# Two products in one 512-column matmul, and modulation sums along VectorE's free axis

## The chip, the cores and the metric

The kernel runs on one NeuronCore of a Trainium2 chip, in one launch. The metric is device time in microseconds (us), the median of several runs of the same program. The engines are called TensorE (PE in the profile, PEld for its weight loads), VectorE (DVE), ScalarE (ACT), GpSimd (POOL) and SyncE (SP, which here issues all loads and stores).

## The reference

Two layers over 256 tokens of width 2048. Each layer takes six modulation vectors from a condition vector, mixes the tokens (layer 0: mLSTM and forgetting attention; layer 1: gated linear attention), and applies a feed-forward block with a convolution over three tokens.

```python
cond = jax.nn.silu(c)
for layer in range(DEPTH):
    mod = (cond @ ada_w[layer] + ada_b[layer])[:, None, :]
    sh_m, sc_m, g_m, sh_f, sc_f, g_f = jnp.split(mod, 6, axis=-1)
    h = rms_norm(x, norm_w[layer, 0]) * (1.0 + sc_m) + sh_m
    y = even_mixer(h, ...) if layer % 2 == 0 else odd_mixer(h, ...)
    x = x + g_m * rms_norm(y, norm_w[layer, 1])
    h = rms_norm(x, norm_w[layer, 2]) * (1.0 + sc_f) + sh_f
    y = conv_ffn(h, ffn_in_w[layer], ffn_conv_w[layer], ffn_conv_b[layer], ffn_out_w[layer])
    x = x + g_f * rms_norm(y, norm_w[layer, 3])

def conv_ffn(h, w_in, conv_w, conv_b, w_out):
    u = h @ w_in                     # 2048 -> 11264
    u = conv over 3 tokens per channel + conv_b
    a, g = jnp.split(u, 2, axis=-1)
    return (a * jax.nn.gelu(g, approximate=True)) @ w_out   # 5632 -> 2048
```

All of it is fp32. `ada_w` is 2 x 2048 x 12288, the largest single weight beside the feed-forward ones.

## The kernel before

Activations lie transposed, channels on the 128 partitions and the 256 tokens (`T`) along the free axis. Every dense product is done with operands split into a high part (rounded to fp32r) and a low part (the remainder): weight-hi times activation-hi, weight-hi times activation-lo, weight-lo times activation-hi. The activation of one channel tile is one row of `act` (or `mid` in the second feed-forward product) with hi in columns 0 to 255 and lo in 256 to 511.

Weights come in 402 units of 1 MB (128 x 2048 floats). A unit of the kinds gates, columns, mixed, ff_up and ff_down is 16 weight tiles of 128 x 128 that make one output tile of 128 channels x 256 tokens; in the last ff_down group of each layer it is 12 tiles. That makes 370 such units; the other 32, of the kind values, use the activations as the stationary operand and 512 weight columns as the moving one. Four raw slots hold loaded units, two slots each of `hi` and `lo` the split ones. For unit n+1 ScalarE writes `hi` (L440, once TensorE has ended unit n-1, whose slot it takes) and VectorE writes `lo` (L806), while TensorE works on unit n. VectorE then evacuates unit n from PSUM (L1186, L1189, L1192; in ff_up the convolution, L1201, L1204 and L1208). Bank 0 and bank 2 alternate.

The order of the work is written out by hand: `PHASES` lists the stages, and in each the loop over units is the same on every engine, in program order. Beside the stages run side jobs (the heads of fox, mlstm and gla), and the modulation: `ada_w` is loaded in 384 pieces of 512 KB, 128 input channels x 1024 outputs each. VectorE multiplies a piece by the 128 conditions (one scalar per partition) and adds it into `acc` (L819 for the first two of a section, L820 for the others). 32 pieces make a section, one of the 12 modulation vectors. Then `reduce_section` sums over the partitions on TensorE, with 16 matmuls of `acc` against a column of ones (L1263), and `close_section` adds the bias (L824). The first 64 pieces are done in a head before the first unit; the others are spread over the units by the tuple `ada` of each stage: one per unit in ff_up (all of layer 0 and the first group of layer 1, 120 units), three per two units in most others, none in the later stages of layer 1. They go through two slots (`piece`).

In ff_up two further engines work on the product: ScalarE applies gelu (L681), GpSimd multiplies (L787), ScalarE rounds to `mid` hi (L685) and GpSimd subtracts (L790) to get `mid` lo.

## Time and profile before

| | |
|---|---|
| median of 3 runs | 2718.58 us (2718.3 to 2723.91) |
| span of the profiled execution | 2725.8 us |
| TensorE busy | 2538.6 us, 93% |
| VectorE busy | 2017.8 us, 74% |
| ScalarE busy | 1076.9 us, 40% |
| GpSimd busy | 460.7 us, 17% |
| loaded | 626.42 MB, 231 GB/s over the span |

The profile is one execution; no total time is given for it apart from its span, which runs from its first to its last instruction. Matmuls overlap each other in the records, so the sum over matmul rows is more than TensorE's busy time, and a matmul's price in a stream is the distance between starts. Other engines' operations are recorded with their duration, and the distance between starts can be a little shorter. "x32" in a row is the number of instructions merged in it.

### The profile page before, as it was taken

Reading aid. Unit: us, or ns where it says so; the run is one execution under the profiler, and the core shown is the slowest. Engines: PE = TensorE matmul, PEld = TensorE weight load, DVE = VectorE, ACT = ScalarE, POOL = GpSimd, SP = SyncE. Lnnn points to the kernel's source line nnn. Section 1 sums busy time; section 2 is a strip of 40 time slices with the busy share of each in tenths; the row PEclk is TensorE's granted clock in tenths of the full one; section 3 lists DMA queues with packets and bytes.
Section 4 is the critical chain, followed back from the end, with each engine's and each line's share of the span. In section 5 each row is a group of like instructions: output and inputs, shape, how many; then the busy total and the mean of one; then the engine's idle time right before and its main releaser. Section 6 shows DMA issues by size and latency. Waiting matters only on the chain.

```text
span 2725.8 us, 48585 instructions
## 1 busy us (share of the span) xinstructions
PE 2538.6 (93%) x19382; PEld 2460.2 (90%) x19382; DVE 2017.8 (74%) x1998; ACT 1076.9 (40%) x1111; POOL 460.7 (17%) x230
## 2 busy tenths in 40 slices
PE   2599998989999999999989999989999999999997
PEld 2498877979999999999988989989899999999997
DVE  7876876789977799688777676667999456645655
ACT  1333334454433333233455544444533334333444
POOL 0100000013420244013301000000344014411320
PEclk7699989989999999999999999989999999999998
DMA  9887764747768767787665644357477455445543
GB/s 394 319 312 272 276 229 147 264 184 263 277 250 309 266 256 276 269 296 261 239 232 215 236 152 151 143 207 272 175 270 265 169 185 185 180 177 183 185 172 137
DMA packets 114640, 630.38 MB, mean 231 GB/s; under 512 B 12736, under 2 KB 12864, under 8 KB 62928
## 3 DMA queue, kind: packets, MB, share of 16 engines
q1 hardware_dynamic: 114512, 628.57, 63.0%
q8 instruction: 93, 1.52, 0.2%
q14 instruction: 35, 0.29, 0.0%
HBM read 626.42 MB, written 2.10 MB: 231 GB/s over the span
## 4 chain that ended last, share of the span: by engine, by line
PE 79%; DVE 9%; DMA 6%; ACT 3%; issue 2%; POOL 0%; DVEq 0%; SPq 0%; ACTq 0%; POOLq 0%
PE bank L1437 23%; PE bank L1438 22%; PE bank L1439 22%; DMA piece<-ada_pieces 4%; DVE acc L820 3%; PE bank L1456 2%; PE bank L1458 2%; PE bank L1457 2%; PE bank L1263 2%; DMA region<-ada_pieces 2%; DVE lo L806 1%; ACT hi L440 1%; PE bank L1341 1%; DVE act L865 1%; PE bank L1256 1%
## 5 line engine op out<-in xcount | busy, mean ns | idle before, releaser
L440 ACT ACTIVATE hi<-raw 128x2048 fp32r<-128x2048 f32 x402 | 769.6, 1915 | 1365.4 <-PE bank L1439 1238.0
L1437 PE MATMUL bank<-act,hi 128*128 128x256 f32 x4384 | 1266.8, 289 | 42.3 <-DVE act L865 26.1
L1438 PE MATMUL bank<-act,hi 128*128 128x256 f32 x4384 | 1252.7, 286 | 0.0
L1439 PE MATMUL bank<-act,lo 128*128 128x256 f32 x4384 | 1252.4, 286 | 0.0
L806 DVE TENSOR_TENSOR lo<-raw,hi 128x2048 fp32r<-128x2048 f32 x402 | 920.2, 2289 | 186.6 <-ACT hi L440 185.4
L1437 PEld LDWEIGHTS bank<-act,hi 128*128 128x128 f32 x4384 | 854.5, 195 | 52.6 <-issue 37.6
L1438 PEld LDWEIGHTS bank<-act,hi 128*128 128x128 f32 x4384 | 854.9, 195 | 1.0
L1439 PEld LDWEIGHTS bank<-act,lo 128*128 128x128 f32 x4384 | 854.0, 195 | 0.0
L820 DVE SCALAR_TENSOR_TENSOR acc<-piece,cond,acc 128x1024 f32<-128x1024 f32 x300 | 436.9, 1458 | 84.3 <-DMA piece<-ada_pieces 83.7
L1437 PE MATMUL bank<-mid,hi 128*128 128x256 f32 x1408 | 408.7, 290 | 12.3 <-POOL mid L790 11.2
L1438 PE MATMUL bank<-mid,hi 128*128 128x256 f32 x1408 | 402.2, 286 | 0.0
L1439 PE MATMUL bank<-mid,lo 128*128 128x256 f32 x1408 | 402.0, 286 | 0.0
L787 POOL TENSOR_TENSOR region<-region 128x256 f32<-128x256 f32 x88 | 201.9, 2294 | 733.4 <-ACT region L681 733.4
L1437 PEld LDWEIGHTS bank<-mid,hi 128*128 128x128 f32 x1408 | 274.4, 195 | 14.4 <-POOL mid L790 12.0
L1438 PEld LDWEIGHTS bank<-mid,hi 128*128 128x128 f32 x1408 | 274.3, 195 | 0.8
L1439 PEld LDWEIGHTS bank<-mid,lo 128*128 128x128 f32 x1408 | 274.1, 195 | 0.0
L790 POOL TENSOR_TENSOR mid<-region,mid 128x256 f32 (+1 forms) x88 | 206.9, 2352 | 291.2 <-ACT mid L685 291.2
L1201 DVE TENSOR_SCALAR region<-bank,vec 128x256 f32<-128x256 f32 x176 | 95.3, 542 | 118.0 <-PE bank L1439 113.3
L743 POOL TENSOR_SCALAR region<-y,mod 128x256 f32<-128x256 f32 x16 | 25.8, 1614 | 557.6 <-DVE y L856 557.6
L1456 PE MATMUL bank<-hi,act 128*128 128x512 f32 x256 | 102.2, 399 | 2.0 <-DVE lo L806 2.0
L1457 PE MATMUL bank<-lo,act 128*128 128x512 f32 x256 | 99.8, 390 | 0.0
L1204 DVE SCALAR_TENSOR_TENSOR region<-bank,vec,region 128x255 f32<-128x255 f32 x176 | 85.0, 483 | 19.9 <-DVE region L1201 1.9
(155 smaller groups left out, 1612.0 us busy)
## 6 DMA issues: line engine op xcount, KB each, us to landing
raw<-w_units SPq DMA_DIRECT2D x402, 1024.0 KB, 4.8
piece<-ada_pieces SPq DMA_DIRECT2D x320, 512.0 KB, 4.9
region<-ada_pieces SPq DMA_DIRECT2D x64, 512.0 KB, 8.6
x<-x_in SPq DMA_DIRECT2D x1, 2048.0 KB, 15.0
x_out<-x SPq DMA_DIRECT2D x4, 512.0 KB, 2.6
vec<-vectors SPq DMA_DIRECT2D x1, 542.5 KB, 3.7
extra<-blocks_in SPq DMA_DIRECT2D x1, 512.0 KB, 18.9
causal<-causal_in SPq DMA_DIRECT2D x1, 256.0 KB, 18.1
```

What stands on the lines that cost most here:

```text
L440: sc.activation(hi[:, slot, :], raw[:, raw_slot, :], ACT.Copy).then_inc(s_hi, 1)
L787: gp.tensor_tensor(ff_m[:, slot, :], conv_a[:, slot, :], gelu_g[:, slot, :], ALU.mult).then_inc(s_mul, 1)
L790: gp.tensor_tensor(flat(mid[:, at_, T:2 * T]), ff_m[:, slot, :], flat(mid[:, at_, 0:T].bitcast(F32)), ALU.subtract).then_inc(s_mid, 1)
L806: ve.tensor_tensor(lo[:, slot, :], raw[:, raw_slot, :], hi[:, slot, :].bitcast(F32), ALU.subtract).then_inc(s_lo, 1)
L820: return ve.scalar_tensor_tensor(out=at_, in0=src, scalar=weight, in1=at_, op0=ALU.mult, op1=ALU.add)
L1201: ve.tensor_scalar(out_, tile_ps, vec[:, bass.ds(ch + 2, 1)], vec[:, bass.ds(ch + 3, 1)], ALU.mult, ALU.add).then_inc(s_v, own.tick())
L1204: ve.scalar_tensor_tensor(out=out_[:, 1:T], in0=tile_ps[:, 0:T - 1], scalar=vec[:, bass.ds(ch + 1, 1)], in1=out_[:, 1:T], op0=ALU.mult, op ...
L1437: pe.matmul(dst, w_hi, src[:, kt, 0:T], start=at == 0, stop=False)
L1438: pe.matmul(dst, w_hi, src[:, kt, T:2 * T], start=False, stop=False)
L1439: i_ = pe.matmul(dst, w_lo, src[:, kt, 0:T], start=False, stop=at == len(order) - 1)
L1456: pe.matmul(dst, x_hi, w_hi, start=kt == 0, stop=False)
L1457: pe.matmul(dst, x_hi, w_lo, start=False, stop=False)
```

## The change

Three things are changed together. In the 370 units that make 128-channel tiles, weight-hi is multiplied with the whole 512-column row of the activation (hi and lo side by side) in one matmul into a whole PSUM bank; weight-lo times activation-hi is added to the first half. The second half is copied to a new tile `low` by ScalarE (`stage_low`) and added by VectorE while it evacuates. Second, the modulation weights are laid out with the output channels on the partitions, `cond` is the condition vector along the free axis, copied to all partitions, and one VectorE operation per piece multiplies and sums into one column of `part`. Third, the one-column matmuls go; `close_section` adds the two halves of each sum and the bias on VectorE.

```diff
-            sc.wait_ge(s_in["vec"], 16)
-            sc.activation(cond[:, :], vec[:, V_C:V_C + DK], ACT.Silu).then_inc(s_cond, 1)
+            sc.wait_ge(s_in["c"], 16)
+            sc.activation(cond[:, :], cond[:, :], ACT.Silu).then_inc(s_cond, 1)
+
+            def stage_low(ph, i, j):
+                t = ph.t0 + j
+                sc.wait_ge(s_unit, SPLIT_SLOTS + unit(ph, i, j) + 1)
+                sc.wait_ge(s_evac, 2 + t + i * ph.tiles)
+                sc.activation(low[:, :], bank[2 * (t % 2)][:, T:2 * T], ACT.Copy).then_inc(s_low, 1)
...
+                        if ph.kind != "values" and not (ph.side == "mlstm" and j == 3):
+                            stage_low(ph, i, j)
...
-            def summed(src, half, kt, first, acc=acc):
-                at_, weight = acc[:, half * PIECE:(half + 1) * PIECE], cond[:, bass.ds(kt, 1)]
-                if first:
-                    return ve.tensor_scalar(at_, src, weight, None, ALU.mult)
-                return ve.scalar_tensor_tensor(out=at_, in0=src, scalar=weight, in1=at_, op0=ALU.mult, op1=ALU.add)
+            def summed(src, half, at_):
+                return ve.scalar_tensor_tensor(out=src, in0=src, scalar=1.0, in1=cond[:, half * PIECE:(half + 1) * PIECE],
+                                               op0=ALU.mult, op1=ALU.mult, accum_out=part[:, bass.ds(at_, 1)])
             def close_section(sec):
-                ve.wait_ge(s_red, sec + 1)
-                ve.tensor_tensor(mod[:, sec, :], bank[7][:, 0:DK], vec[:, V_ADAB + sec * DK:V_ADAB + (sec + 1) * DK],
+                two = part[:, sec % 2 * PIECES:(sec % 2 + 1) * PIECES].rearrange("p (k two) -> p k two", two=2)
+                ve.wait_ge(s_mac, (sec + 1) * PIECES)
+                ve.tensor_tensor(mod[:, sec, :], two[:, :, 0], two[:, :, 1], ALU.add).then_inc(s_pair, 1)
+                ve.wait_ge(s_pair, sec + 1)
+                ve.tensor_tensor(mod[:, sec, :], mod[:, sec, :], vec[:, V_ADAB + sec * DK:V_ADAB + (sec + 1) * DK],
                                  ALU.add).then_inc(s_mod, 1)
...
-                        ve.wait_ge(s_mac, a - 1)
...
                         elif ph.kind == "columns":
-                            ve.tensor_copy(region[:, bass.ds((ph.dest + ph.units * i + j) * T, T)], tile_ps)\
+                            ve.tensor_tensor(region[:, bass.ds((ph.dest + ph.units * i + j) * T, T)], tile_ps, low[:, :],
+                                             ALU.add).then_inc(s_evac, 1)
...
                         elif ph.kind == "ff_down":
                             at_ = flat(y[:, bass.ds(4 * i + j, 1), :])
-                            ve.tensor_tensor(at_, at_, tile_ps, ALU.add).then_inc(s_evac, 1)
+                            ve.tensor_tensor(low[:, :], at_, low[:, :], ALU.add).then_inc(s_v, own.tick())
+                            mine()
+                            ve.tensor_tensor(at_, tile_ps, low[:, :], ALU.add).then_inc(s_evac, 1)
                         elif ph.kind == "ff_up":
...
-                            ve.tensor_scalar(out_, tile_ps, vec[:, bass.ds(ch + 2, 1)], vec[:, bass.ds(ch + 3, 1)],
+                            ve.tensor_tensor(low[:, :], tile_ps, low[:, :], ALU.add).then_inc(s_v, own.tick())
+                            mine()
+                            ve.tensor_scalar(out_, low[:, :], vec[:, bass.ds(ch + 2, 1)], vec[:, bass.ds(ch + 3, 1)],
                                              ALU.mult, ALU.add).then_inc(s_v, own.tick())
                             mine()
-                            ve.scalar_tensor_tensor(out=out_[:, 1:T], in0=tile_ps[:, 0:T - 1],
+                            ve.scalar_tensor_tensor(out=out_[:, 1:T], in0=low[:, 0:T - 1],
...
-            def reduce_section(sec, acc=acc):
-                if sec > 0:
-                    pe.wait_ge(s_mod, sec)
-                pe.wait_ge(s_mac, (sec + 1) * PIECES)
-                for j in range(DK):
-                    i_ = pe.matmul(bank[7][:, j:j + 1], acc[:, j * P:(j + 1) * P], ones[:, 0:1], start=True, stop=True)
-                i_.then_inc(s_red, 1)
...
-                        pe.matmul(dst, w_hi, src[:, kt, 0:T], start=at == 0, stop=False)
-                        pe.matmul(dst, w_hi, src[:, kt, T:2 * T], start=False, stop=False)
-                        i_ = pe.matmul(dst, w_lo, src[:, kt, 0:T], start=False, stop=at == len(order) - 1)
+                        pe.matmul(both, w_hi, src[:, kt, :], start=at == 0, stop=False)
+                        i_ = pe.matmul(both[:, 0:T], w_lo, src[:, kt, 0:T], start=False, stop=at == len(order) - 1)
...
-    ada = ada_w.reshape(LAYERS, DK, P, 6, 2, PIECE).transpose(0, 3, 1, 4, 2, 5).reshape(-1, P, PIECE)
+    ada = ada_w.reshape(LAYERS, 2, PIECE, 6, DK, P).transpose(0, 3, 4, 1, 5, 2).reshape(-1, P, PIECE)
```

Left out: the copy of c is now the first load (1 MB, from one row of 8 KB), and `vec` comes after the head's first eight pieces; VectorE waits for `low` (`s_low`) before an evacuation, not for TensorE; the phases count their column units; the other evacuations are changed like the one shown.

The program's order on VectorE in ff_up with a piece, before, from one split (`lo`) to the next; region is where the convolution's result lies:

```order
L806 TENSOR_TENSOR lo<-raw,hi 128x2048
L820 SCALAR_TENSOR_TENSOR acc<-piece,cond,acc 128x1024
L1201 TENSOR_SCALAR region<-bank,vec 128x256
L1204 SCALAR_TENSOR_TENSOR region<-bank,vec,region 128x255
L1208 SCALAR_TENSOR_TENSOR region<-bank,vec,region 128x254
```

and at the same place after the change:

```order
L818 TENSOR_TENSOR lo<-raw,hi 128x2048
L829 SCALAR_TENSOR_TENSOR piece,part<-piece,cond 128x1024
L1218 TENSOR_TENSOR low<-bank,low 128x256
L1220 TENSOR_SCALAR region<-low,vec 128x256
L1223 SCALAR_TENSOR_TENSOR region<-low,vec,region 128x255
L1227 SCALAR_TENSOR_TENSOR region<-low,vec,region 128x254
```

Five operations are six now, and the last three read `low` instead of the bank.

On ScalarE, in the straight part at the end of an ff_up stage, before (hi is a split, the L681 row a gelu):

```order
L440 ACTIVATE hi<-raw 128x2048
L681 ACTIVATE region<-region 128x256
L440 ACTIVATE hi<-raw 128x2048
L685 ACTIVATE mid<-region 128x256
L440 ACTIVATE hi<-raw 128x2048
```

and after:

```order
L442 ACTIVATE hi<-raw 128x2048
L691 ACTIVATE region<-region 128x256
L686 ACTIVATE low<-bank 128x256
L442 ACTIVATE hi<-raw 128x2048
L695 ACTIVATE mid<-region 128x256
L686 ACTIVATE low<-bank 128x256
L442 ACTIVATE hi<-raw 128x2048
```

Each unit has a `low` copy, behind gelu or the rounding and ahead of the split of the unit after next.

On TensorE, inside an ff_up stage of layer 0 where a section ends, before (ones is the column of ones, acc the sums):

```order
L1437 MATMUL bank<-act,hi 128x256
L1438 MATMUL bank<-act,hi 128x256
L1439 MATMUL bank<-act,lo 128x256
L1263 MATMUL bank<-ones,acc 128x1 x16
L1437 MATMUL bank<-act,hi 128x256
```

After the change the rows named L1263 are gone, and every tile reads (here the first two tiles of the first unit):

```order
L1443 MATMUL bank<-act,hi 128x512
L1444 MATMUL bank<-act,lo 128x256
L1443 MATMUL bank<-act,hi 128x512
L1444 MATMUL bank<-act,lo 128x256
```

## Rows read from the trace of the kernel before

**Rows 1.** The page's busy time per engine, share of the span and instructions.

```profile
PE 2538.6 (93%) x19382; PEld 2460.2 (90%) x19382; DVE 2017.8 (74%) x1998; ACT 1076.9 (40%) x1111; POOL 460.7 (17%) x230
```

**Rows 2.** Stretches: length, busy PE, PEld, DVE, ACT, POOL, PEclk, DMA, GB/s.

```profile
642.00:665.00 23.00, 23.00 (x194) 23.00 (x193) 21.58 (x21) 9.06 (x9) 9.48 (x4) 1.00 0.74 274
2206.00:2390.00 184.00, 184.00 (x1536) 184.00 (x1535) 118.64 (x125) 71.23 (x62) 69.16 (x29) 1.00 0.50 182
```

**Rows 3.** Timeline of ScalarE, two units of columns and two of values: start, duration.

```profile
129.31 1.92 ACT L440 ACTIVATE hi<-raw 128x2048 fp32r<-128x2048 f32 x1 [3.84 <-PE bank L1439]
135.07 1.92 ACT L440 ACTIVATE hi<-raw 128x2048 fp32r<-128x2048 f32 x1 [3.84 <-PE bank L1439]
...
234.88 1.92 ACT L440 ACTIVATE hi<-raw 128x2048 fp32r<-128x2048 f32 x1 [3.52 <-PE bank L1458]
240.32 1.92 ACT L440 ACTIVATE hi<-raw 128x2048 fp32r<-128x2048 f32 x1 [3.52 <-PE bank L1458]
```

**Rows 4.** Groups by line and shape: count, busy us, mean ns, idle before.

```profile
L1437 PE MATMUL bank<-act,hi 128*128 128x256 f32 x4384 | 1266.8, 289 | 42.3 <-DVE act L865 26.1 <-DVE act L1082 12.7 <-DVE lo L806 3.2
L1437 PE MATMUL bank<-mid,hi 128*128 128x256 f32 x1408 | 408.7, 290 | 12.3 <-POOL mid L790 11.2 <-DVE lo L806 1.1
L1189 DVE COPY y<-bank 128x256 f32 x40 | 16.9, 423 | 27.8 <-PE bank L1439 27.8
L1192 DVE TENSOR_TENSOR y<-y,bank 128x256 f32<-128x256 f32 x32 | 13.4, 420 | 35.0 <-PE bank L1439 35.0
L934 DVE TENSOR_SCALAR region<-region,stat 128x256 f32<-128x256 f32 x24 | 7.4, 350 | 0.4
L594 ACT ACTIVATE region<-bank 128x256 f32<-128x256 f32 x4 | 1.5, 374 | 1.3 <-PE bank L1268 1.3
L1003 DVE CUSTOM_DVE_ANT_0 region<-region,bank 128x256 f32<-128x256 f32 x8 | 3.0, 416 | 0.0
L1003 DVE DVE_READ_ACCUMULATOR2_ANT stat<- 128x1 f32 x8 | 0.7, 84 | 0.0
```

**Rows 5.** The one-column matmuls: their group, and those of one section end.

```profile
L1263 PE MATMUL bank<-ones,acc 128*128 128x1 f32 x352 | 52.7, 284 | 29.0 <-DVE acc L820 29.0
...
940.30 4.19 PE L1263 MATMUL bank<-ones,acc 128*128 128x1 f32 x32 [0.41 <-DVE acc L820]
```

**Rows 6.** Waits: total us, times, longest us.

```profile
PE bank L1263 <- DVE acc L820: 29.0, 8, 22.2
DVE mod L824 <- PE bank L1263: 19.1, 8, 4.3
```

**Rows 7.** Timeline of VectorE: a unit of ff_up in the loop; below, straight code.

```profile
649.26 2.28 DVE L806 TENSOR_TENSOR lo<-raw,hi 128x2048 fp32r<-128x2048 f32 x1
651.46 1.76 DVE L820 SCALAR_TENSOR_TENSOR acc<-piece,cond,acc 128x1024 f32<-128x1024 f32 x1
653.20 0.55 DVE L1201 TENSOR_SCALAR region<-bank,vec 128x256 f32<-128x256 f32 x1
653.89 0.48 DVE L1204 SCALAR_TENSOR_TENSOR region<-bank,vec,region 128x255 f32<-128x255 f32 x1
654.52 0.48 DVE L1208 SCALAR_TENSOR_TENSOR region<-bank,vec,region 128x254 f32<-128x254 f32 x1
654.99 2.29 DVE L806 TENSOR_TENSOR lo<-raw,hi 128x2048 fp32r<-128x2048 f32 x1
...
934.32 0.53 DVE L1201 TENSOR_SCALAR region<-bank,vec 128x256 f32<-128x256 f32 x1
934.89 0.48 DVE L1204 SCALAR_TENSOR_TENSOR region<-bank,vec,region 128x255 f32<-128x255 f32 x1
```

**Rows 8.** Timeline of GpSimd beside that unit.

```profile
649.73 2.41 POOL L790 TENSOR_TENSOR mid<-region,mid 128x256 f32 x1 [3.37 <-ACT mid L685]
```

**Rows 9.** Timeline of the head: ScalarE's Silu, VectorE's sums.

```profile
4.47 0.22 ACT L676 ACTIVATE cond<-vec 128x16 f32<-128x16 f32 x1 [2.46 <-DMA vec<-vectors]
21.98 28.04 DVE L820 SCALAR_TENSOR_TENSOR acc<-region,cond,acc 128x1024 f32<-128x1024 f32 x22 [5.34 <-DMA region<-ada_pieces]
```

More of the change, by code:

```diff
@@ L75, in place @@
         pairs += 2 * self.bodies if self.kind == "ff_up" else 0
-        return self.end, t + self.bodies * self.tiles, self.a_end, pairs
+        c += 0 if self.kind == "values" else self.bodies * self.units
+        return self.end, t + self.bodies * self.tiles, self.a_end, pairs, c
     def straight(self, i):
@@ L139 @@
 REGION = V_AT + TB * D
-OWN = {("ff_up", None): 8, ("columns", "fox"): 6, ("values", "fox"): 12, ("columns", "mlstm"): 14,
+OWN = {("ff_up", None): 12, ("columns", "fox"): 6, ("values", "fox"): 12, ("columns", "mlstm"): 14,
        ("values", "gla"): 8, ("columns", "gla"): 8}
@@ L223, in program @@
         ident = sb("ident", [P, P])
-        ones = sb("ones", [P, T])
+        ones = sb("ones", [P, P])
+        low = sb("low", [P, T])
         causal = sb("causal", [P, TB, T])
@@ L1152, in sum_piece @@
                         a = ph.a0 + i * ph.per_body + k
-                        done = (ph.a0 + ph.now * ph.per_body + k) % PIECES - ph.now * ph.per_body
-                        first = isinstance(a, int) and a % PIECES < 2
-                        if first and a % PIECES == 0 and (k > 0 or ph.side == "mlstm" or not first_body(i)):
+                        first = isinstance(a, int) and a % PIECES == 0
+                        if first and (k > 0 or ph.side == "mlstm" or not first_body(i)):
                             close_section(a // PIECES - 1)
@@ L1174, in body @@
                         tile_ps = bank[2 * (tile_no % 2)][:, 0:T]
-                        if ph.kind != "values" or j % 4 == 3:
+                        if ph.kind != "values":
+                            ve.wait_ge(s_low, ph.c0 + i * ph.units + j + 1)
+                        elif j % 4 == 3:
                             ve.wait_ge(s_unit, SPLIT_SLOTS + n + 1)
@@ L1214, in body @@
                         k += ph.ada[j]
-                per = OWN.get((ph.kind, ph.side), 0)
+                per = ph.units if ph.kind == "ff_down" and ph.group > 0 else OWN.get((ph.kind, ph.side), 0)
                 roots_per = 2 if ph.side == "mlstm" else 0
@@ L1416, in columns @@
                     pe.wait_ge(s_evac, ph.t0 + i * ph.tiles + j + 1)
-                    dst = bank[2 * ((ph.t0 + j) % 2)][:, 0:T]
+                    both = bank[2 * ((ph.t0 + j) % 2)][:, :]
                     src = mid if ph.kind == "ff_down" else act
@@ L1467, in body @@
                             {"fox": fox_work, "mlstm": mlstm_work, "decay": decay_work, "gla": gla_work}[ph.side](ph, i, j)
-                        a = ph.a0 + i * ph.per_body + sum(ph.ada[:j])
-                        if isinstance(a, int):
-                            for last in range(a, min(a + ph.ada[j], ph.a_end - 1)):
-                                if last % PIECES == PIECES - 1:
-                                    reduce_section(last // PIECES)
                         if ph.sums and not (first_body(i) and j == 0):
@@ L1589 @@
         "ada_pieces": np.ascontiguousarray(ada),
+        "c_row": np.ascontiguousarray(c),
         "vectors": vec,
```

56 lines of the change are left out of this document (24 added, 32 removed).

## The prediction

> **What bounds the kernel now.** I read the page's busy line first, then a table of stretches, then single units, then the operations one by one. The busy line gives TensorE 2538.6 us of 2725.8 [rows 1], so what TensorE has to stream is the first suspect, and a second engine has to be looked for stage by stage. The stretches do that [rows 2]. In the ff_up stage of layer 1 without modulation pieces TensorE is busy for all 184 us, VectorE for 118.6: TensorE bounds it, with a third of VectorE to spare. In the ff_up stage of layer 0, where every unit also sums a piece, TensorE is busy all the time too, but VectorE 21.58 of 23.00, 94%. There two engines are within 6% of each other, and work moved from one to the other shows at once.
>
> The unit times say what TensorE's stream costs. ScalarE's split of the unit after next starts when TensorE ends a unit. In the columns stage these starts lie 5.76 us apart, with 48 matmuls of 256 columns each: 120.0 ns a matmul. In the values stage they lie 5.44 us apart, with 24 matmuls of 512 columns: 226.7 ns [rows 3]. The same 12,288 columns go through in both, so a matmul costs 13.3 ns beside its columns, at the full clock.
>
> **Part 1, the merged matmul.** One 512-column matmul takes the place of two of 256: per weight tile 226.7 + 120.0 = 346.7 ns for 360.0, 13.3 less. A unit of 16 tiles goes from 5.76 to 5.55 us (0.21 less), one of 12 tiles loses 0.16. There are 4384 + 1408 = 5792 tiles [rows 4], 77 us in all, if TensorE bounds every unit. It doesn't:
> - 88 units of layer 1's ff_up and ff_down without pieces are bound by TensorE alone, 18.8 us; the 32 of 12 tiles give 5.1 us.
> - 96 units of the stages with three pieces in two units, and 34 of gates, fox, mlstm and gla, give 27.7 us if TensorE bounds them. Some wait for a piece to land, or for ScalarE and VectorE in a side job, so I take half, 13.8.
> - 120 units of ff_up with a piece (88 of layer 0, 32 of layer 1) give nothing; part 3 shows why.
>
> Together -37.7 us. The price of a mixed pair isn't in the trace; between nothing saved (a pair costs 360) and the 13.3 of a uniform stream I take the latter.
>
> By the Trainium skill ("TensorE: Matmul & The Clock Gate", section "Wait — 56ns, not 53.3ns?") a warm matmul costs only about 2.5 ns beside its columns. By that, all 5792 merges would be worth 14 us and the sum would end some 30 us higher. The rows show 13.3 ns here, and the measurement decides.
>
> **Part 2, the one-column matmuls.** A section's reduction is 16 of them, recorded as 32, and it stands in TensorE's stream: at 940.30 it takes 4.19 us, with 0.41 us of waiting for VectorE's last piece in front. Over eleven sections they are busy 52.7 us [rows 5], 4.8 each; I take 4.6, between the two rows. One of the eleven lies in the head, where TensorE has nothing else to do, and two (the ends of the mixed stages) beside the norm's own chain; there I count nothing. The other eight give 37 us. The waits in front are 29.0 us, of which the longest, 22.2, is the head's; 6.8 are left. VectorE in turn waits up to 4.3 us to close a section [rows 6], so neither engine covers the other and the time is real. -44 us. What replaces them is one more 128x16 add on VectorE, no more than 0.4 us a section with its wait.
>
> **Part 3, the evacuation.** The two correction products now lie in two halves of a bank, and someone has to add them. ScalarE copies the second half to `low` (a PSUM copy of 256 took 374 ns, L594 in [rows 4]), and VectorE adds. For columns, mixed and the first ff_down group the add replaces a copy that costs the same (423 ns against 420 for an add with one input in PSUM). In ff_down's later groups there is one more add. In ff_up there is one more add and one more wait in the chain of four.
>
> The ff_up unit with a piece, start to start now [rows 7]: 2.20 (split) + 1.74 (piece) + 0.69 + 0.63 + 0.47 = 5.73 us, which fills TensorE's 5.76. The piece takes 1.76 rather than 1.28 us, because GpSimd's add, started 0.47 us after the split, ends 0.68 us after the piece began [rows 7, 8]. Afterwards: an add of 0.42 plus the 0.15 that a dependent step waits in such a loop, +0.57. The `tensor_scalar` reads SBUF in place of PSUM (350 ns in L934 against 550), -0.19. The two others read SBUF, and their 480 ns is their price with a scalar from memory; unchanged. 5.73 + 0.57 - 0.19 = 6.11, and 0.04 for a collision now and then: 6.15 us. That is more than 5.55 and more than 5.76: VectorE becomes the bound, and 0.39 us x 120 units = +47 us. Bounds: if the waits cost only the 0.04 us seen in straight code (last two of [rows 7]), 5.95 us, +23. If every second unit's GpSimd add now collides a second time (its `mid` subtraction falls beside two-input SBUF operations, which it didn't before) for another 0.48, and the accumulator is read out for 0.08, 6.45 us, +83.
>
> The piece operation itself: it loses the scalar in memory and gains an accumulator. The nearest row is L1003, 416 ns for 256 elements and 84 ns for reading the accumulator, but the next one starts while it is read. I take no change for 1.28 us; from -0.06 to +0.25 as bounds, and a doubling is a rival below.
>
> **Part 4, what grows in latency.** ScalarE's `low` stands in front of the split of the unit after next: TensorE end, 0.4 for `low`, 1.92 split, 2.29 low part, near 4.8 us; through VectorE in ff_up 0.5 + 2.2 + 2.3 = 5.0. Both are below 5.55, so in a stage bound by TensorE this hides behind the unit in between, with 0.5 us to spare. Where TensorE waits for the end of a chain it doesn't hide. From ff_up to ff_down (six times, TensorE waits there for GpSimd's `mid`, 11.2 us by the second row of [rows 4]): `low` 0.5 and the extra add 0.4, +5.4 us. At the norms (four times) 0.5 to 1.05, +3. In fox, mlstm and gla, whose side jobs share ScalarE and VectorE, I put +5, from 0 to 15.
>
> **Part 5, the head.** The sums start when a 128-row copy of c has landed (1 MB) and after a Silu over 2048 elements (1.9 us by the split's row) instead of 0.22. VectorE then runs without a gap, 22 pieces of 0.52 MB in 28.04 us [rows 9], 1.27 us each, so the shift stays. At that rate of 411 GB/s 1 MB takes 2.6 us, and the first pieces of the two sections, simple products now, cost up to 0.5 us more each, less what the dropped waits give. +4 us, from 0 to 10.
>
> **The sum.** -37.7 - 44 + 47 + 5.4 + 3 + 5 + 4 = -17.3 us, against the profiled span of 2725.8 us: 2708.5. The span is 7.2 us above the median of the runs (2718.58) and 1.9 above the slowest; the same difference off the median gives 2701.
>
> **Rivals.**
> - A, VectorE holds up: the dependent steps in ff_up cost what straight code shows, the sums get faster without their waits, and the period with a piece is near 5.8 us. For: in straight code L1204 starts 0.57 us after L1201, in the loop 0.69 [rows 7]. Against: 94% busy before anything is added. Then part 3 costs 5, not 47: about 2660.
> - B, slower: GpSimd and VectorE collide in the evacuation. Before, three of VectorE's five operations read PSUM and left GpSimd alone; now three of them take SBUF operands that collide. Place: the 120 ff_up units. Price: 6.45 us a unit, +83; with part 1 at 30 it ends at 2745. It decides from 6.28 us a unit on, where the gain is gone.
> - C, the accumulator halves the sum: 1024 elements take 1.28 us and 255 take 0.48 [rows 7, 9], so streaming 1024 costs 1.07 us, and at half the rate a piece would take 2.35 us. 120 ff_up units +128, 60 head pieces +64, and the fox stage's two pieces a unit some more: about 2920. Against: L820 reads two fp32 tensors of SBUF now at one element a cycle. The Trainium skill speaks for it ("Vector Engine (DVE) Microarchitecture Reference", section "Points that are easy to get wrong"): this form "with two non-bf16 SBUF sources halves throughput", for want of a port for the accumulator. The present row, without accumulator, isn't halved; no row shows it with one.
> - D, the merge saves nothing, because the weight load behind a 256-column matmul isn't hidden when a 512-column one follows: part 1 is 0, about 2740.
>
> **Chances.** Forecast 0.46 (2701, own range 2680 to 2725), A 0.22, B 0.18, C 0.06, D 0.08. A measurement of this kernel tells 0.2%, 5.4 us, from no change. Faster by more than that (below 2713): A, and three quarters of the forecast's share, 0.22 + 0.35, with a little of D: 0.58. Within 0.2%: 0.13. Slower: B, C, most of D, the tail of the forecast: 0.29. The range goes from A's 2660 to above B, 2755; beyond it lie C and the ends of A and B.
>
> **What would show it.** In the profile after: 512-column matmuls and 256-column ones alternating, 5.55 us a unit in layer 1's ff_up without pieces and 6.1 to 6.2 with one, TensorE idle there before each unit and VectorE near 100%. No reduction at the section ends. `low` copies of 0.37 us on ScalarE. The head about 4 us longer. The pieces at 1.28 us outside ff_up. I am wrong if the units with a piece stay at 5.8 or less, if they pass 6.3, if the unit without a piece isn't below 5.7, or if a piece takes over 1.5 us outside ff_up.

## The result, and the profile after

| | before | after |
|---|---|---|
| median | 2718.97 us (2718.3 to 2723.91, 4 runs) | 2682.46 us (2677.95 to 2690.78, 4 runs) |
| span of the profiled execution | 2725.8 us | 2676.1 us |

The ratio is 0.9867, with a 95% interval of 0.9848 to 0.9885: 36.5 us or 1.3% faster, where 17.3 us were forecast. The sign was right and the time lies in the range, but the size is off by more than a factor of two, and as will be seen the terms are off by more than the sum.

The busy line of the page and two stretches, columns as in [rows 1] and [rows 2]: a piece of ff_up with modulation in layer 0, then the ff_up stage of layer 1 without pieces.

```profile
PE 2430.7 (91%) x13206; PEld 2067.7 (77%) x13206; DVE 2085.3 (78%) x2634; ACT 1187.2 (44%) x1481; POOL 362.5 (14%) x230
```

```profile
620.00:643.00 23.00, 22.20 (x125) 18.71 (x124) 21.06 (x27) 10.32 (x12) 5.55 (x4) 1.00 0.69 248
2160.00:2343.00 183.00, 180.85 (x1025) 156.19 (x1024) 130.26 (x156) 81.16 (x94) 58.23 (x29) 1.00 0.52 184
```

TensorE has a third fewer matmuls and 108 us less busy time, but the median fell by a third of that. In both stretches, where it never stood still before [rows 2], it now has gaps.

The groups that answer to [rows 4], and the sums:

```profile
L1443 PE MATMUL bank<-act,hi 128*128 128x512 f32 x4384 | 1572.7, 402 | 142.5 <-DVE act L879 98.7
L829 DVE SCALAR_TENSOR_TENSOR piece<-piece,cond 128x1024 f32<-128x1024 f32 x320 | 425.7, 1331 | 68.5 <-DMA piece<-ada_pieces 68.2
L686 ACT ACTIVATE low<-bank 128x256 f32<-128x256 f32 x370 | 142.4, 385 | 1052.6 <-PE bank L1444 1052.6
```

VectorE in a loop of ff_up with a piece, two units, which answers to [rows 7]:

```profile
625.20 2.29 DVE L818 TENSOR_TENSOR lo<-raw,hi 128x2048 fp32r<-128x2048 f32 x1
627.40 1.76 DVE L829 SCALAR_TENSOR_TENSOR piece<-piece,cond 128x1024 f32<-128x1024 f32 x1
629.09 0.08 DVE L829 DVE_READ_ACCUMULATOR piece<-piece,cond  x1
629.09 0.41 DVE L1218 TENSOR_TENSOR low<-bank,low 128x256 f32<-128x256 f32 x1
629.70 0.41 DVE L1220 TENSOR_SCALAR region<-low,vec 128x256 f32<-128x256 f32 x1 [0.19 <-DVE low L1218]
630.25 0.49 DVE L1223 SCALAR_TENSOR_TENSOR region<-low,vec,region 128x255 f32<-128x255 f32 x1
630.89 0.92 DVE L1227 SCALAR_TENSOR_TENSOR region<-low,vec,region 128x254 f32<-128x254 f32 x1
631.73 2.28 DVE L818 TENSOR_TENSOR lo<-raw,hi 128x2048 fp32r<-128x2048 f32 x1
633.93 1.21 DVE L829 SCALAR_TENSOR_TENSOR piece<-piece,cond 128x1024 f32<-128x1024 f32 x1
```

One unit takes 6.53 us, the next 5.69; the mean over such loops is 5.99. Beside them GpSimd (compare [rows 8]):

```profile
625.89 2.19 POOL L799 TENSOR_TENSOR region<-region 128x256 f32<-128x256 f32 x1 [6.12 <-ACT region L691]
630.79 0.74 POOL L802 TENSOR_TENSOR mid<-region,mid 128x256 f32 x1 [2.71 <-ACT mid L695]
```

VectorE's operation that starts while GpSimd (L799 its multiplication, L802 its subtraction) is at work is lengthened: the piece from 1.21 to 1.76 us by the multiplication, the last step from 0.48 to 0.92 by the subtraction, both in the same unit. The `lo` at 625.20, which had started before the multiplication, keeps its 2.29; there it is GpSimd's operation that is recorded with 2.19 us, where the subtraction, which started outside a long operation, has 0.74. The next unit is undisturbed. Straight code, at a stage's end, has the same operations closer together:

```profile
901.40 0.41 DVE L1218 TENSOR_TENSOR low<-bank,low 128x256 f32<-128x256 f32 x1
901.85 0.42 DVE L1220 TENSOR_SCALAR region<-low,vec 128x256 f32<-128x256 f32 x1
902.30 0.48 DVE L1223 SCALAR_TENSOR_TENSOR region<-low,vec,region 128x255 f32<-128x255 f32 x1
902.82 0.48 DVE L1227 SCALAR_TENSOR_TENSOR region<-low,vec,region 128x254 f32<-128x254 f32 x1
903.22 2.29 DVE L818 TENSOR_TENSOR lo<-raw,hi 128x2048 fp32r<-128x2048 f32 x1
```

The four steps start 0.45, 0.45 and 0.52 us apart here, 0.61, 0.55 and 0.64 in the loop.

TensorE's stream in the ff_up stage without pieces, the first and the last pair of two stretches in which it never stands still, and the wait between them:

```profile
2198.08 0.40 PE L1443 MATMUL bank<-act,hi 128*128 128x512 f32 x1
2198.32 0.28 PE L1444 MATMUL bank<-act,lo 128*128 128x256 f32 x1
...
2219.99 0.40 PE L1443 MATMUL bank<-act,hi 128*128 128x512 f32 x1
...
2220.74 0.49 PE L1443 MATMUL bank<-act,hi 128*128 128x512 f32 x1 [0.24 <-DVE lo L818]
...
2221.18 0.40 PE L1443 MATMUL bank<-act,hi 128*128 128x512 f32 x1
...
2242.68 0.40 PE L1443 MATMUL bank<-act,hi 128*128 128x512 f32 x1
```

A stretch has 63 pairs here, so 62 distances: 353.4 ns a pair in the first, 346.8 in the second. A pair has two levels, and which one it has changes where TensorE stood still. Of the 134 unbroken stretches of 14 and more pairs in this execution 128 keep one level from end to end, among them one of 394 pairs. Of the pairs in these stretches 57% lie at the upper level and 39% at the lower.

The stage reaches neither 5.65 us a unit (16 pairs at 353.4) nor 5.55 (at 346.8): its 32 units take 183.6 us, 5.74 each. The rows that show why:

```profile
2283.66 0.39 ACT L686 ACTIVATE low<-bank 128x256 f32<-128x256 f32 x1 [2.31 <-PE bank L1444]
2284.19 0.43 DVE L1218 TENSOR_TENSOR low<-bank,low 128x256 f32<-128x256 f32 x1 [1.16 <-ACT low L686]
...
2286.43 0.74 POOL L802 TENSOR_TENSOR mid<-region,mid 128x256 f32 x1 [2.80 <-ACT mid L695]
2286.48 2.84 DVE L818 TENSOR_TENSOR lo<-raw,hi 128x2048 fp32r<-128x2048 f32 x1
...
2289.44 0.50 PE L1443 MATMUL bank<-act,hi 128*128 128x512 f32 x1 [0.35 <-DVE lo L818]
```

From the end of TensorE's unit at 2283.6 it goes through `low` and four dependent steps (only the first is shown) to a `lo` that ends at 2289.3, 5.7 us later; it takes 2.84 us instead of 2.29 because GpSimd's subtraction had started 0.05 us before it. TensorE, done with the unit in between, has waited 0.35 us for it. This happens in about every fourth unit, seven times in the stage. From one such wait to the next, four units, it is 23.1 us where the pairs have the upper level and 22.8 where they have the lower, for 22.6 and 22.2 of stream.

Where the time went, from the profiled executions of both and of the main experiments; a stage goes from its first weight-lo subtraction on VectorE to the next stage's first (us):

| | before | after | sums only | sums only, straight | after, straight | last version |
|---|---|---|---|---|---|---|
| head | 97.0 | 99.1 | 99.0 | 98.9 | 98.6 | 99.1 |
| mixer stages (12) | 958.5 | 932.1 | 933.7 | 938.5 | 933.4 | 936.1 |
| ff_up with a piece (4) | 763.7 | 766.3 | 747.0 | 746.8 | 742.4 | 734.5 |
| ff_up without (2) | 322.6 | 321.9 | 322.5 | 322.6 | 320.2 | 313.0 |
| ff_down (6) | 584.0 | 556.6 | 564.4 | 563.6 | 554.1 | 553.4 |
| span | 2725.8 | 2676.1 | 2666.8 | 2670.5 | 2648.7 | 2636.1 |

These are single executions. The one before lies about 7 us above its median, the one after the change 4.5 below, "after, straight" 7.1 below and "sums only, straight" 4.5 above theirs; "sums only" and the last version lie within 0.5 us of theirs. So a few us between two columns say little, least in the mixer and ff_down rows. ff_up without pieces is the steadiest row: 322.5 or 322.6 us in all three executions without the merge.

### The profile page after: what moved, and what is told of

It reads as the page before. It is cut to its first block, busy times and chain, and to the rows that moved or that the text cites. A ratio compares the mean times of both kernels' runs of the same rounds, so it can differ in the third digit from the quotient of the medians.

```text
span 2676.1 us, 37876 instructions
## 1 busy us (share of the span) xinstructions
PE 2430.7 (91%) x13206; PEld 2067.7 (77%) x13206; DVE 2085.3 (78%) x2634; ACT 1187.2 (44%) x1481; POOL 362.5 (14%) x230
## 4 chain that ended last, share of the span: by engine, by line
PE 55%; DVE 27%; issue 9%; ACT 3%; DMA 3%; DVEq 1%; POOL 1%; ACTq 0%; SPq 0%; POOLq 0%
PE bank L1443 29%; PE bank L1444 15%; DVE lo L818 9%; DVE piece L829 4%; DVE region L1223 2%; DVE region L1220 2%; PE bank L1461 2%; PE bank L1462 2%; PE bank L1463 2%; DVE low L1218 2%; DMA piece<-ada_pieces 1%; DVE region L829 1%; DMA region<-ada_pieces 1%; PE bank L1350 1%; PE bank L1275 1%
## 5 line engine op out<-in xcount | busy, mean ns | idle before, releaser
L1443 PE MATMUL bank<-act,hi 128*128 128x512 f32 x4384 | 1572.7, 402 | 142.5 <-DVE act L879 98.7
L1443 PEld LDWEIGHTS bank<-act,hi 128*128 128x128 f32 x4384 | 828.7, 189 | 365.4 <-issue 148.8
L686 ACT ACTIVATE low<-bank 128x256 f32<-128x256 f32 x370 | 142.4, 385 | 1052.6 <-PE bank L1444 1052.6
L1443 PE MATMUL bank<-mid,hi 128*128 128x512 f32 x1408 | 509.9, 406 | 19.7 <-POOL mid L802 19.1
L829 DVE SCALAR_TENSOR_TENSOR piece<-piece,cond 128x1024 f32<-128x1024 f32 x320 | 425.7, 1331 | 68.5 <-DMA piece<-ada_pieces 68.2
L1443 PEld LDWEIGHTS bank<-mid,hi 128*128 128x128 f32 x1408 | 268.2, 191 | 87.9 <-POOL mid L802 21.0
L799 POOL TENSOR_TENSOR region<-region 128x256 f32<-128x256 f32 x88 | 195.2, 2218 | 865.4 <-ACT region L691 865.4
L802 POOL TENSOR_TENSOR mid<-region,mid 128x256 f32 (+1 forms) x88 | 115.6, 1313 | 236.6 <-ACT mid L695 236.6
L1227 DVE SCALAR_TENSOR_TENSOR region<-low,vec,region 128x254 f32<-128x254 f32 x176 | 99.1, 563 | 19.9 <-DVE region L1223 0.9
L1461 PE MATMUL bank<-hi,act 128*128 128x512 f32 x256 | 103.3, 404 | 2.9 <-DVE lo L818 2.9
L1463 PE MATMUL bank<-hi,act 128*128 128x512 f32 x256 | 100.7, 394 | 0.0
L1223 DVE SCALAR_TENSOR_TENSOR region<-low,vec,region 128x255 f32<-128x255 f32 x176 | 85.2, 484 | 19.9 <-DVE region L1220 2.6
```

The source lines that it names most:

```text
L686: sc.activation(low[:, :], bank[2 * (t % 2)][:, T:2 * T], ACT.Copy).then_inc(s_low, 1)
L799: gp.tensor_tensor(ff_m[:, slot, :], conv_a[:, slot, :], gelu_g[:, slot, :], ALU.mult).then_inc(s_mul, 1)
L829: return ve.scalar_tensor_tensor(out=src, in0=src, scalar=1.0, in1=cond[:, half * PIECE:(half + 1) * PIECE], op0=ALU.mult, op1=ALU.mult, a ...
L1223: ve.scalar_tensor_tensor(out=out_[:, 1:T], in0=low[:, 0:T - 1], scalar=vec[:, bass.ds(ch + 1, 1)], in1=out_[:, 1:T], op0=ALU.mult, op1=AL ...
L1443: pe.matmul(both, w_hi, src[:, kt, :], start=at == 0, stop=False)
L1461: pe.matmul(dst, x_hi, w_hi, start=kt == 0, stop=False)
```

## The experiments

All were timed beside the kernel before; the ratios are to it.

### The two halves of the change, apart

e1: the new modulation sums, and the matmuls and evacuations of before.

```diff
-                        pe.matmul(both, w_hi, src[:, kt, :], start=at == 0, stop=False)
+                        pe.matmul(both[:, 0:T], w_hi, src[:, kt, 0:T], start=at == 0, stop=False)
+                        pe.matmul(both[:, 0:T], w_hi, src[:, kt, T:2 * T], start=False, stop=False)
```

> The new modulation sums without the merged matmul: three 256-column matmuls a tile and the old evacuation, no low copy. Theory S (the gain is the reductions', and more than I forecast: near 55 us of TensorE time and stalls, less 4 in the head; the merge as a whole costs some 10 to 15 us): 2664 to 2674 us, faster than the change itself. Rival M (the two halves share the gain, the merge brings near 15 us by itself): 2695 to 2700.

Measured: 2668.70 us (2664.84 to 2669.75), ratio 0.981 (0.9788 to 0.9832).

e2: the kernel before with the 512-column matmuls, `low` and its adds, and the old sums and one-column matmuls.

> The merged matmul with the old sums into acc and the one-column matmuls. Theory S: not faster than before, 2720 to 2735 us; a plain ff_up unit at 5.65 us, one with a piece near 6.1 in the loops. Rival M: 2700 to 2705, and the two parts' differences from before add up to the change's -36.

Measured: 2738.29 us (2736.19 to 2748.60), ratio 1.0069 (1.0049 to 1.0088).

The sums alone bring 51.5 us, the merge alone costs 18, together they bring 37. The theory that the sums carry the gain stands. The merge loses, by about what the prediction's terms for it add up to, but these terms are to be looked at one by one.

### Who pays for the merge

e3: the changed kernel, with VectorE's code of the four ff_up stages with a piece written out instead of looped. No operation changes.

```diff
+                kept, ph.head = ph.head, ph.bodies if ph.kind == "ff_up" and ph.per_body > 0 else ph.head
                 repeat(ve, ph, counted)
+                ph.head = kept
```

> The change with VectorE's ff_up stages with a piece written out straight instead of looped (the other engines keep their loops; same operations in the same order). Theory L (a dependent step costs 0.12 to 0.16 us more in a loop than in straight code, and VectorE bounds these units): all 120 units at 5.71 us as the 40 that are straight now, some 80 x 0.28 = 22 us less, about 2660. Rival G (the 5.54/6.44 alternation in the loops comes from GpSimd's two collisions with VectorE, and the order stays): within 5 us of the change, 2680.

Measured: 2657.56 us (2650.49 to 2670.07), ratio 0.978 (0.9753 to 0.9808): theory L. Nearly every unit with a piece now takes 5.71 to 5.72 us. The rows of one:

```profile
624.27 2.29 DVE L818 TENSOR_TENSOR lo<-raw,hi 128x2048 fp32r<-128x2048 f32 x1
626.47 1.76 DVE L829 SCALAR_TENSOR_TENSOR piece<-piece,cond 128x1024 f32<-128x1024 f32 x1
...
629.99 2.28 DVE L818 TENSOR_TENSOR lo<-raw,hi 128x2048 fp32r<-128x2048 f32 x1
```

VectorE has no idle time in it, and the period is above the 5.55 to 5.65 of TensorE's stream, so VectorE still sets it. The 0.55 us of GpSimd now fall on the piece in nearly every unit. Where they don't (in 46 units of e12, below), a unit takes 5.17 us. So both the loop and GpSimd keep VectorE behind TensorE; only the loop was taken out here.

e5: the changed kernel, with the 120 units of ff_up with a piece as in e1, the rest merged.

> The change, but the 120 ff_up units that sum a piece keep the three 256-column matmuls and the old evacuation. Theory V (VectorE bounds these units with the extra add): they go back to 5.76 from 5.99 in loops and 5.71 in straight code, 80 x 0.23 - 40 x 0.05 = 16 us less, near 2666. Rival T (TensorE's saving in these units is real and pays for the add): 2682 or more.

Measured: 2668.25 us (2660.52 to 2679.48), ratio 0.9805 (0.9782 to 0.9829). Both remedies work, so the loss is VectorE's in these units.

e11: the changed kernel without the extra add. The convolution reads the bank again, and the kernel leaves the product of weight-hi with activation-lo out of ff_up's result.

```diff
-                            ve.tensor_tensor(low[:, :], tile_ps, low[:, :], ALU.add).then_inc(s_v, own.tick())
-                            mine()
-                            ve.tensor_scalar(out_, low[:, :], vec[:, bass.ds(ch + 2, 1)], vec[:, bass.ds(ch + 3, 1)],
+                            ve.tensor_scalar(out_, tile_ps, vec[:, bass.ds(ch + 2, 1)], vec[:, bass.ds(ch + 3, 1)],
```

> The changed kernel with the extra add in ff_up left out: the convolution reads the bank, and the product of weight-hi with activation-lo is left out of ff_up's result. ScalarE's copy of the second half stays. Theory V (the add and its dependent wait are what makes VectorE the bound in ff_up's loops, 5.99 us a unit in 80 units): the loops go to TensorE's 5.65 to 5.70, 23 to 28 us less, straight units 5.71 to 5.65 and the stages without pieces 5.75 to 5.65, 5 us more: 2648 to 2656. Rival C (the loop's period is made by the collisions between GpSimd and the piece, not by the add): 2668 or more.

Measured: 2645.39 us (2634.35 to 2658.29), ratio 0.9713 (0.9687 to 0.974). Theory V, and a little more: -37 us. Layer 1's ff_up with a piece, the changed kernel first, then e11, in the columns of [rows 2]:

```profile
1920.00:2040.00 120.00, 113.69 (x640) 97.49 (x639) 110.01 (x141) 51.56 (x60) 29.09 (x21) 1.00 0.72 261
```

```profile
1910.00:2020.00 110.00, 110.00 (x625) 95.36 (x624) 103.93 (x120) 51.54 (x60) 45.76 (x19) 1.00 0.76 278
```

With the add TensorE has 6.3 us of gaps in 120, without it none. VectorE shows 92% in the first row and is nevertheless what TensorE waits for: the rest is the time between dependent steps. GpSimd's collisions with the piece did not go away (105 of the 120 pieces are lengthened in e11, 61 with the add), so they alone don't make TensorE wait. But e11 takes three things out at once, the add, its wait, and the reads of `low` in SBUF beside which the subtraction fell (39 last steps lengthened with the add, none without). It prices them together.

e6: e1 with VectorE straight in the same stages.

> The new sums alone, with VectorE's code of the ff_up stages with a piece written out without a loop, as the fastest kernel so far (2657.6) has it, but without the merged matmuls. Theory T (without the merge TensorE bounds these units at 5.76 us, VectorE has slack, so straight code gives nothing): 2666 to 2672, and the fastest kernel owes its 11 us over the new sums to the merge, which pays once VectorE keeps up. Rival Q (straight code is faster by itself): 2655 to 2662, and the merge is worth nothing even there.

Measured: 2667.92 us (2664.24 to 2672.42), ratio 0.9809 (0.9789 to 0.983). Straight code is worth nothing where TensorE is the bound. So the difference of e3 to e6, 10.4 us, is what the merge brings with VectorE straight; the intervals of the two ratios overlap a little (e13, below, gives 8.1).

### What the one-column matmuls cost

e7: e1 with an idle reduction at each section end.

```diff
+            def idle_reduction():
+                for j in range(DK):
+                    pe.matmul(bank[7][:, j:j + 1], cond[:, j * P:(j + 1) * P], ones[:, 0:1], start=True, stop=True)
```

> The kernel with the new sums alone, and with 16 one-column matmuls put back at each of the section ends, which wait for nothing, read the condition vector and whose results nobody reads: the stream of the old reduction without its waits. Theory P (the old reduction cost what its matmuls take in TensorE's stream): 8 sections by 4.2 to 4.6 us, +34 to +37 on the 2668.7 of the new sums alone: 2702 to 2706, and nearly all of the 51 us is explained. Rival W (most of it was the two waits around the matmuls, TensorE for VectorE's last sum and VectorE for the closing): under +20, 2675 to 2688.

Measured: 2706.97 us (2699.09 to 2708.86), ratio 0.9948 (0.9928 to 0.9967): 38.3 us over e1, just above theory P's range. Its reason, that this is what the matmuls take, is only part of it: the 16 matmuls hold TensorE's stream only from 933.43 to 936.92, 3.49 us, and eight times that is 28. For the rest the granted clock is the candidate. A section end in the kernel before, the one of [rows 5]:

```profile
940.00:944.00 4.00, 3.69 (x31) 3.73 (x31) 3.64 (x5) 2.21 (x2) 1.71 (x1) 0.92 0.93 360
944.00:950.00 6.00, 6.00 (x29) 6.00 (x29) 1.06 (x3) 0.00 (x0) 0.81 (x1) 0.50 0.72 273
950.00:956.00 6.00, 6.00 (x52) 6.00 (x51) 2.56 (x4) 2.22 (x2) 0.70 (x1) 0.99 0.00 0
```

The eighth column is the granted clock as a share: behind the reduction TensorE runs at 0.50, the lower of its levels, for 6 us, and 29 matmuls lie there where the next 6 us hold 52. That is nearly 3 us lost at this section end, on top of the 4.19 of the reduction.

e10: the same idle reduction with 64 columns instead of one.

```diff
-                    pe.matmul(bank[7][:, j:j + 1], cond[:, j * P:(j + 1) * P], ones[:, 0:1], start=True, stop=True)
+                    pe.matmul(bank[7][:, 0:64], cond[:, j * P:(j + 1) * P], ones[:, 0:64], start=True, stop=True)
```

> As the kernel with the new sums and an idle reduction at the section ends, but each of its 16 matmuls has 64 columns instead of one. The one-column kind took 3.5 us at a section end and left TensorE at a granted clock of 0.50 for about 3 us behind it; it cost 38.3 us in all. Theory K (it is the near-empty stream that brings the clock down): with 64 columns the 16 matmuls take 3.5 to 4.5 us, the clock stays at 1.00 behind them, and the cost falls to 28 to 34 us: 2697 to 2703. Rival N (the clock has nothing to do with the columns, or the price is by the column): 2705 or more.

Measured: 2691.25 us (2689.48 to 2693.47), ratio 0.9895 (0.9877 to 0.9914): 22.6 us over e1, below what theory K allowed, and 15.7 less than with one column. The same place in e7 and in e10, the reduction and what follows, and the clock there:

```profile
933.43 3.63 PE L1299 MATMUL bank<-ones,cond 128*128 128x1 f32 x32
936.92 0.36 PE L1473 MATMUL bank<-act,hi 128*128 128x256 f32 x1
...
937.00:939.00 2.00, 2.00 (x13) 2.00 (x13) 1.97 (x4) 0.00 (x0) 1.52 (x1) 0.65 0.49 180
939.00:941.00 2.00, 2.00 (x12) 2.00 (x11) 0.90 (x2) 0.00 (x0) 0.00 (x0) 0.50 0.78 311
```

```profile
925.55 3.68 PE L1299 MATMUL bank<-ones,cond 128*128 128x64 f32 x32
929.04 0.36 PE L1473 MATMUL bank<-act,hi 128*128 128x256 f32 x1
...
929.00:931.00 2.00, 2.00 (x19) 2.00 (x18) 1.97 (x4) 0.00 (x0) 1.64 (x1) 1.00 0.38 156
931.00:933.00 2.00, 2.00 (x19) 2.00 (x18) 1.02 (x2) 0.00 (x0) 0.00 (x0) 1.00 0.88 291
```

Both reductions hold the stream for 3.49 us; after the one of 64 columns the clock stays at 1.00. The 15.7 us are the price of the lower clock behind one-column matmuls (14.4 by the ratios, as the two were timed apart), and the 22.6 that are left are the price of the held stream. In e7 the level of 0.50 behind the eight section ends that count lasts 37.5 us in all, half of which is lost; in e10 none of the eight has it. The 11.6 us between e7 and the kernel before that ran beside it (2718.58) are what the old sums cost beside the matmuls. The same places have 47.8 us at 0.50 there, so an estimate is 5 us of clock and 6.5 of waits [rows 6]. That the clock stays low longer because of the waits is not shown: the five ends with 6.8 us of it or more do have a wait of 0.41 us or more in front, but so has one with 3.4, and three ends of e7 have 6.8 without any wait.

### The order inside a unit

e4: the changed kernel with a unit's 16 matmuls of 512 columns first, then its 16 of 256.

> The changed kernel, but in each unit the 16 matmuls of 512 columns (weight-hi) come first and the 16 of 256 (weight-lo) after them, instead of in turns. In the changed kernel a pair costs 353.3 ns, 6.7 more than 226.7 + 120.0. Theory X: the 6.7 ns are the price of alternating lengths; in runs of one length a unit takes 5.55 us where TensorE bounds it, in about 150 units, 0.10 each: 2662 to 2672. Rival Y: the price belongs to a matmul with a weight load of its own, whatever its neighbours: units stay at 5.65 and the time at 2677 to 2684.

Measured: 2697.08 us (2685.23 to 2699.79), ratio 0.9906 (0.9884 to 0.9929), slower than the changed kernel. Plain units went to 5.57 us, about as theory X has it (though pairs in turns reach 5.55 too, at their lower level), but both theories missed the time: the first units of the stages, which take their activation tiles as they arrive, got slower. In ff_up with a piece in layer 1 (224.2 us, 218.4 in the changed kernel) the first two units take 45.6 us for 39.9, and the others 178.6 for 178.5, by the starts of `lo`; in the ff_down stages the second unit takes 8.8 to 11.1 us for 7.1 to 7.9.

e8: e4, and TensorE waits for `lo` only before the 256-column half.

```diff
-                        pe.wait_ge(s_lo, RAW_SLOTS + unit(ph, i, j) + 1)
+                        pe.wait_ge(s_hi, unit(ph, i, j) + 1)
...
+                    pe.wait_ge(s_lo, RAW_SLOTS + unit(ph, i, j) + 1)
+                    for at, kt in enumerate(order):
```

> As the kernel with all 512-column matmuls first, and TensorE starts a unit when weight-hi is there and waits for weight-lo only before the second half. Theory L (in the ff_up stages without pieces, 56 units at 5.75 where TensorE's stream is 5.65 or less, and at the norms and the ff_down starts, TensorE waits for the chain low copy, VectorE's four operations, lo part; 3.6 us more time for the chain removes this): 8 to 18 us below the kernel without the late wait, and ff_up without pieces at the unit time of TensorE's stream. Rival M (the wait only moves to the middle of the unit, or VectorE's total work bounds): within 4 us of it.

Measured: 2669.87 us (2663.56 to 2678.54), ratio 0.9817 (0.9793 to 0.9841): 27 us below e4, more than theory L. The ff_up stages without pieces took 312.7 us, after 320.0 in e4 and 321.9 in the changed kernel: the chain shown above was what TensorE waited for there. Another 17.1 us came in the stages with a piece (775.5 to 758.4, by the two profiled executions).

e9: e8 with VectorE straight as in e3.

> The kernel with the 512-column matmuls first and the late wait for weight-lo, and VectorE's code of the ff_up stages with a piece written out without a loop. Theory A (the two add up: straight code took 19 to 25 us off the loops, the late wait 5 to 8 us off the ff_up stages without pieces): 2645 to 2655, below the fastest so far (2657.6). Rival B (the gaps at the starts of the ff_down and norm stages and the lower clock after them, which this order shows more of, eat it): 2657 to 2668.

Measured: 2655.29 us (2651.85 to 2657.41), ratio 0.9762 (0.9744 to 0.9781): the upper edge of theory A. Its stages show both: ff_up without pieces 312.7 us (e3: 320.2), ff_down 566.3 (554.1).

e12: e9, but the first unit of a stage takes the two lengths in turns.

```diff
+                        if first_body(i) and j == 0:
+                            i_ = pe.matmul(both[:, 0:T], w_lo, src[:, kt, 0:T], start=False, stop=at == len(order) - 1)
+                    if not (first_body(i) and j == 0):
+                        pe.wait_ge(s_lo, RAW_SLOTS + unit(ph, i, j) + 1)
```

> A version that takes each order where it did best: 512-column matmuls first and the late wait for weight-lo in all units, except a stage's first, where the two lengths go in turns because the activation tiles arrive one by one; VectorE straight in the ff_up stages with a piece. Theory A (with all 512-column matmuls first TensorE takes the arriving tiles at 227 ns each and then stands still, where turns give it 347 ns of work per tile: ff_down stages of 94 to 95 us against 91 to 93): 8 to 12 us below the 2655.3 of the version with that order everywhere, 2643 to 2648. Rival B (the ff_down stages are longer for another reason, the order within all their units): 2652 to 2658.

Measured: 2638.35 us (2627.97 to 2645.72), ratio 0.9702 (0.9678 to 0.9727), the fastest of all and 5 us below theory A's range. ff_down is back at 553.4 us. 80 us below the kernel before, 44 below the changed one. The chain of waits on its page, by engine:

```profile
PE 49%; DVE 33%; DMA 10%; issue 4%; ACT 3%; POOL 1%; DVEq 0%; SPq 0%; ACTq 0%; POOLq 0%
```

e13: e3 once more.

> The changed kernel with VectorE straight in the ff_up stages with a piece, run once more beside the last version. In its first run (2657.6) a pair of matmuls took 353.3 ns in layer 0 and 346.7 in layer 1's later stages, where the changed kernel needs 353.3 throughout. Theory D (this belongs to the program, to where its code lies): 2650 to 2662 again, and again 346.7 ns in layer 1. Rival E (it belongs to the execution): other stages, or none, show 346.7 ns.

Measured: 2659.80 us (2648.56 to 2662.21), ratio 0.9772 (0.975 to 0.9793). The time is e3's. The first and the last pair of the unbroken stretch that starts in the same ff_down stage of layer 1, in e3 (331 pairs) and in e13 (336):

```profile
2331.57 0.40 PE L1445 MATMUL bank<-mid,hi 128*128 128x512 f32 x1
...
2445.98 0.39 PE L1445 MATMUL bank<-act,hi 128*128 128x512 f32 x1
```

```profile
2336.32 0.40 PE L1445 MATMUL bank<-mid,hi 128*128 128x512 f32 x1
...
2454.70 0.40 PE L1445 MATMUL bank<-act,hi 128*128 128x512 f32 x1
```

That is 346.7 ns a pair in e3 and 353.4 in e13; in the stage before it is 346.7 in both. One program, one stage, two levels: not theory D, and nearer to theory E. It isn't the execution as a whole either, as the two stretches of the changed kernel above show: the level belongs to a stretch between two standstills. What at the standstill sets it isn't known.

## Why the prediction was right in sign and wrong in size

**Part 2 (one-column matmuls, -44) was too small.** e1 brings 51.5 us although its head is 2.0 us longer, so the term is about -53.5. The step that failed is the price of a section: it was read from the reduction's own row, 4.6 us, 37 for eight, and the clock behind it was put at nothing. The granted clock stays at 0.50 there, and by e7 and e10 that costs 15.7 us. The held stream cost 22.6, less than the 37, and the waits with what they bring 11.6 for 6.8. So a term that was left out was partly made up for by one that was too large.

**Part 1 (the merge, -37.7) was the largest error.** Two of its steps failed. The pair was put at 346.7 ns throughout, and about three in five have 353.4: the prediction named this as unmeasured, and took the favourable end of 0 to 13.3. On all pairs it is at most 23 us, and less where TensorE doesn't bound. And the stages that were called bound by TensorE alone stopped being so: ff_up without pieces gave 0.7 us (322.6 to 321.9) for 11.8 forecast. There part 4 had put the chain through VectorE at 5.0 us against 5.55 and called it hidden. Without disturbance that is nearly so (0.57 + 2.29 + 2.29 by the rows above, 5.15 us); but where GpSimd's subtraction falls on the weight-lo subtraction it is 5.7, and the 0.5 us to spare are gone. A collision of this kind stood in [rows 7, 8], and the prediction had counted it in part 3 only. Of the 9.2 us that e8 gains in these stages, 7.3 are this wait (320.0 to 312.7). Outside the stages with a piece parts 1 and 4 were forecast at -24.3 together; by the profiled executions the merge gave 10.0 there.

**Part 3 (VectorE in ff_up, +47) had the right mechanism and place, and was too large.** Against e1 the four stages are 19.3 us longer (766.3 to 747.0). The period of the loops is 5.99 us for 6.15 forecast, and about 40 of the 120 units lie in straight code, where it is 5.72. The prediction used both prices as alternatives, when both kinds of code are in these stages. The piece itself takes 1.21 us, below the 1.28 kept; its accumulator read is overlapped. e11 puts the add, its wait and the reads of `low`, in every ff_up stage, at 37 us, e3 and e13 the part that comes from the loops at 23 to 25. Three small slips change nothing: the lower bound adds up to 6.00 us, not 5.95, the gain is gone from 6.29 us a unit, not 6.28, and what [rows 8] show is GpSimd's subtraction, not an add.

**Together.** The merge's terms were forecast at -37.7 + 47 + 13.4 (part 4) = +22.7; measured it is 13.8 by the medians (2682.46 to 2668.70). The sums were forecast at -40 with the head; measured -51.5. The errors inside the merge, a gain too large and a cost too large, partly cancelled, which is luck; what remains of the miss is 11.5 us of the sums and 8.9 of the merge.

**The head (+4)** took 2.1 us. The other terms of part 4 have no run of their own.

**The rivals.** A (VectorE holds up) is wrong in the loops; with straight code (e3) the time comes out near A's 2660, at 2657.6, though VectorE still sets the period of 5.71 there. B: the collisions come as described, but only in every second unit, and 5.99 isn't 6.45. C: the Trainium skill's rule of a halved rate ("Vector Engine (DVE) Microarchitecture Reference", "Points that are easy to get wrong") doesn't show here; with an accumulator and two fp32 sources in SBUF 1024 elements took 1.21 us. D is partly true: in the stretches at 353.4 ns half of the saving is missing. Whether the weight load is the reason the runs leave open.

## What to carry to other kernels

Price an interruption of TensorE's stream by the granted clock in the microseconds behind it too, not by its own rows alone. Before moving work from the bounding engine to the next one, compute the second engine's period including what dependent steps wait, and know which units run in loops and which straight, and which of its operations can start while GpSimd is at work. When one operand is ready earlier than the other, order the matmuls so that the late one is needed last, except where inputs arrive tile by tile.

## What the runs showed of the hardware

- 16 fp32 matmuls of one column and of 64 columns each hold TensorE for 3.49 us. After the first the granted clock was 0.65 in the next 2 us and 0.50 in the 2 after them, after the second 1.00; over the kernel that made 15.7 us.
- The same dependent steps on VectorE start 0.55 to 0.64 us apart in a loop and 0.45 to 0.52 in straight code; over the 80 units in loops that was 23 to 25 us (e3 and e13 against the changed kernel), and nothing where TensorE bounds (e6).
- A pair of a 512- and a 256-column matmul in turns took 346.7 or 353.4 ns. The level differed between e3 and e13 in the same stage and between neighbouring stretches of one stage; 128 of 134 stretches without a standstill kept theirs.
- GpSimd's operations of 256 elements lengthened a VectorE operation on SBUF that started while they ran: the multiplication the piece by 0.55 us (1.21 to 1.76), the subtraction `lo` by 0.55 (2.29 to 2.84) and the last step by 0.44 (0.48 to 0.92). A GpSimd operation that started inside `lo` was itself recorded with 2.19 us instead of 0.74.
